# Latent expansion of the second block: three products ahead, one total per tile, stores from the sync engine

## The chip, the cores and the metric

The kernel runs on one core of a Trainium2 chip. The metric is the device time of one execution in microseconds. Five engines take part: TensorE (PE, with PEld for its weight loads), VectorE (DVE), ScalarE (ACT), GpSimd (POOL) and the sync engine (SP), which only issues DMAs here. A name with a q (ACTq, SPq) is an issue of a DMA by that engine.

## The reference, cut to what matters

The program is two transformer blocks over 1024 tokens of width 1024. The change touches one part of the second block, the expansion of the latent attention's queries and keys (four heads):

```python
q = (_rmsnorm_2(c_q, q_a_norm_w) @ w_uq).reshape(b, s, MLA_HEADS, MLA_QK)       # MLA_QK = 128 + 64
q_nope, q_rope = q[..., :MLA_NOPE], q[..., MLA_NOPE:]
q_rope = q_rope * cos + _rotate_half(q_rope) * sin
kv = (_rmsnorm_2(c_kv, kv_a_norm_w) @ w_ukv).reshape(b, s, MLA_HEADS, MLA_NOPE + MLA_V)
k_nope, v_mla = kv[..., :MLA_NOPE], kv[..., MLA_NOPE:]
k_rope = broadcast over the heads of (k_rope * cos + _rotate_half(k_rope) * sin)
q_m = _rmsnorm_2(concatenate([q_nope, q_rope]), mla_q_norm_w)
k_m = _rmsnorm_2(concatenate([k_nope, k_rope]), mla_k_norm_w)
o_mla = _mla_attention(q_m, k_m, v_mla)
```

So each of the eight (head, query or key) pairs needs a product of 128 features x 1024 tokens, the sum of squares over its 128 plain and 64 rotated features, the inverse root of that sum, and two scalings.

## The kernel before

All engines run programs of their own and meet at semaphores. Everything is laid out features first: a tile is 128 partitions (features) x 1024 tokens. Float32 products are made of three rounded products (high x high, low x high, high x low; lines 523 to 525), so a tile with one K block is 6 matmuls of 512 columns and one with two K blocks is 12. PSUM is used as four slots of 128 x 1024, `wide(0)` to `wide(3)`.

The stage before this one makes the rotated parts of the queries (`q_rope`, two tiles, each with two heads) and of the keys (`k_rope`), and the values `v_value`; ACT issues the stores of the values (line 1524), then squares the two tiles of `q_rope` (line 1527). `k_rope_sq` was made earlier.

The latent expansion then runs over e = 0 to 7: head e // 2, key tile for even e (one K block, weights `ukv`), query tile for odd e (two K blocks, weights `uq_nope`).

- TensorE: `expand(e)` makes the product in slot e % 2; from e = 2 it waits until tile e - 2 has been scaled out of it (`g_free`). `head_total(e)` adds over the features with a matrix of ones: the squared product `tmp[e % 2]`, and then the rotated squares with a matrix that picks 64 partitions (`halves`), into slot 2 + e % 2 (line 561). The order is product 0, then total 0, product 1, total 1, product 2 and so on.
- ACT: `head_square(e)` (line 1535) squares the product; then come the logarithm of the total (line 1549) and its exponential (line 1555), which give the inverse root `g_rms`. Between these, ACT issues the stores of tile e - 1 (lines 1541 and 1542) and does the square of e + 1.
- DVE: scales the product out of PSUM to `g_nope` (line 2018) and the rotated part to `g_rope` (line 2022). From e = 2 on it waits for the store of tile e - 2, which used the same buffer.
- SP: after the weight slabs it waits for the stores of the values and of both parts of head 0 (`g_stored[e] >= 32 * hd + 32`), and loads head 0 from memory into `head_raw` in seven DMAs (line 380); the loads of the next heads follow as POOL has split the ones before.
- POOL: when all seven have landed, ten operations split head 0 into high and low parts (lines 496 and 500).

The attention starts when head 0 is split (TensorE, `logits(0)`, ten matmuls a unit) and when all stores of the expansion have landed (DVE waits for `g_stored` at 128 ahead of its first maximum, line 2029).

## Time and profile before

| | us |
|---|---|
| median of the runs (lowest, highest) | 3333.71 (3331.11, 3339.38) |
| the profiled execution | 3333.93 |
| its span | 3332.1 |
| TensorE, busy in the span | 3149.4 (95%) |
| DVE | 1506.8 (45%) |
| POOL | 1176.7 (35%) |
| ACT | 824.1 (25%) |
| share of TensorE in the chain that ended last | 88% |
| latent expansion, from the first value store (2114.76) to the first maximum (2192.62) | 77.9 |

The span is the time from the first to the last instruction of the core. A busy TensorE is not a TensorE at its peak; its granted clock is told as a share of 2.4 GHz (0.50 is 1.2 GHz), its mean over the span is 0.977. The chain that ended last goes back from the last instruction, at each step to what released it. In a row by stretch stand its start and end, its length, the busy time of PE, PEld, DVE, ACT and POOL with the number of instructions, the mean granted clock, the share of time that the DMA engines were busy (of 1), and GB/s. The share of an engine in the whole span says little on this stage: the rows of the stage itself are what is to be read.

### The profile page before, as it was taken

Reading aid. Unit: us, or ns where it says so; the run is one execution under the profiler, and the core shown is the slowest. Engines: PE = TensorE matmul, PEld = TensorE weight load, DVE = VectorE, ACT = ScalarE, POOL = GpSimd, SP = SyncE. Lnnn points to the kernel's source line nnn. Section 1 sums busy time; section 2 is a strip of 40 time slices with the busy share of each in tenths; the row PEclk is TensorE's granted clock in tenths of the full one; section 3 lists DMA queues with packets and bytes.
Section 4 is the critical chain, followed back from the end, with each engine's and each line's share of the span. In section 5 each row is a group of like instructions: output and inputs, shape, how many; then the busy total and the mean of one; then the engine's idle time right before and its main releaser. Section 6 shows DMA issues by size and latency. Waiting matters only on the chain.

```text
span 3332.1 us, 34809 instructions
## 1 busy us (share of the span) xinstructions
PE 3149.4 (95%) x13566; PEld 2462.9 (74%) x13566; DVE 1506.8 (45%) x2220; ACT 824.1 (25%) x1194; POOL 1176.7 (35%) x559
## 2 busy tenths in 40 slices
PE   7999998999988899999999799889998999999999
PEld 5788785678765688888887477568666788888887
DVE  3799956554443522121223521355984423223226
ACT  3322205511334201001001332245774100001001
POOL 2254333334422234334333133273002444444443
PEclk9899999999999999999999899999999999999999
DMA  2022310034200011111111122442421111111112
GB/s 104 26 89 96 141 48 7 1 131 157 78 26 26 26 51 47 48 50 45 50 50 44 34 86 97 139 139 67 111 83 60 39 51 48 47 50 45 49 50 76
DMA packets 69272, 217.54 MB, mean 65 GB/s; under 512 B 7468, under 2 KB 18900, under 8 KB 68408
## 3 DMA queue, kind: packets, MB, share of 16 engines
q1 hardware_dynamic: 40832, 145.51, 14.1%
q10 hardware_dynamic: 28344, 70.74, 5.8%
q8 instruction: 62, 1.02, 0.1%
q14 instruction: 34, 0.28, 0.0%
HBM read 175.31 MB, written 40.65 MB: 65 GB/s over the span
## 4 chain that ended last, share of the span: by engine, by line
PE 88%; DVE 5%; ACT 4%; issue 1%; POOL 1%; ACTq 0%; DMA 0%; POOLq 0%; DVEq 0%
PE ps L523 26%; PE ps L525 25%; PE ps L524 25%; PE ps L561 3%; PE ps L724 2%; PE ps L1047 1%; PE ps L1035 1%; PE ps L714 1%; PE ps L1020 1%; POOL w_lo L419 1%; DVE x L1720 1%; DVE y L1719 1%; PE ps L1021 1%; POOL w_hi L416 0%; ACT mprobs L1423 0%
## 5 line engine op out<-in xcount | busy, mean ns | idle before, releaser
L416 POOL TENSOR_TENSOR w_hi<-w_raw,zero 128x1024 fp32r<-128x1024 f32 x202 | 385.4, 1908 | 1785.5 <-PE ps L525 1778.8
L523 PE MATMUL ps<-normed_hi,w_hi 128*128 128x512 f32 x1488 | 588.5, 395 | 34.7 <-DVE normed_lo L1704 18.2
L524 PE MATMUL ps<-normed_lo,w_hi 128*128 128x512 f32 x1488 | 583.6, 392 | 0.0
L525 PE MATMUL ps<-normed_hi,w_lo 128*128 128x512 f32 x1488 | 583.1, 392 | 0.0
L419 POOL TENSOR_TENSOR w_lo<-w_raw,w_hi 128x1024 fp32r<-128x1024 f32 x202 | 537.6, 2661 | 15.9
L523 PEld LDWEIGHTS ps<-normed_hi,w_hi 128*128 128x128 f32 x1488 | 282.2, 190 | 100.4 <-issue 28.6
L523 PE MATMUL ps<-hidden_hi,w_hi 128*128 128x512 f32 x864 | 336.9, 390 | 2.8 <-DVE hidden_lo L1944 2.8
L525 PE MATMUL ps<-hidden_hi,w_lo 128*128 128x512 f32 x864 | 336.8, 390 | 0.0
L524 PE MATMUL ps<-hidden_lo,w_hi 128*128 128x512 f32 x864 | 336.6, 390 | 0.0
L524 PEld LDWEIGHTS ps<-normed_lo,w_hi 128*128 128x128 f32 x1488 | 282.2, 190 | 60.6 <-issue 2.2
L525 PEld LDWEIGHTS ps<-normed_hi,w_lo 128*128 128x128 f32 x1488 | 282.1, 190 | 59.3
L523 PE MATMUL ps<-h_hi,w_hi 128*128 128x512 f32 x528 | 208.8, 395 | 8.3 <-DVE h_lo L1704 5.0
L524 PE MATMUL ps<-h_lo,w_hi 128*128 128x512 f32 x528 | 207.6, 393 | 0.0
L525 PE MATMUL ps<-h_hi,w_lo 128*128 128x512 f32 x528 | 207.4, 393 | 0.0
L1942 DVE TENSOR_TENSOR tmp<-tmp,ps 128x1024 f32<-128x1024 f32 x22 | 26.9, 1221 | 369.0 <-PE ps L525 367.5
L523 PEld LDWEIGHTS ps<-hidden_hi,w_hi 128*128 128x128 f32 x864 | 162.6, 188 | 37.0 <-DVE hidden_lo L1944 3.2
L525 PEld LDWEIGHTS ps<-hidden_hi,w_lo 128*128 128x128 f32 x864 | 162.5, 188 | 33.9
L524 PEld LDWEIGHTS ps<-hidden_lo,w_hi 128*128 128x128 f32 x864 | 162.6, 188 | 33.7
L2156 DVE TENSOR_TENSOR y<-y,ps 128x1024 f32<-128x1024 f32 x64 | 78.1, 1220 | 206.6 <-PE ps L525 205.6
L1778 DVE MATCH_REPLACE8 score<-top,score 128x1024 f32<-128x1024 f32 (+2 forms) x192 | 167.9, 889 | 0.0
L1774 DVE MAX8 top<-score 128x8 f32<-128x1024 f32 (+2 forms) x192 | 162.2, 893 | 0.0
L2148 DVE TENSOR_TENSOR tmp<-tmp 128x1024 f32<-128x1024 f32 x32 | 59.6, 1861 | 220.1 <-ACT tmp L1678 220.1
(366 smaller groups left out, 5171.5 us busy)
## 6 DMA issues: line engine op xcount, KB each, us to landing
w_raw<-weights_dram SPq DMA_DIRECT2D x228, 512.0 KB, 3.6
gates_scratch<-tmp ACTq DMA_DIRECT2D x24, 512.0 KB, 2.7
gated<-gates_scratch ACTq DMA_DIRECT2D x24, 512.0 KB, 5.6
head_part<-diff_qk_scratch SPq DMA_DIRECT2D x48, 256.0 KB, 6.4
x_in<-x_dram ACTq DMA_DIRECT2D x4, 1024.0 KB, 10.9
x<-x_dram ACTq DMA_DIRECT2D x1, 4096.0 KB, 14.6
diff_qk_scratch<-d_hi ACTq DMA_DIRECT2D x8, 512.0 KB, 2.7
diff_qk_scratch<-d_out ACTq DMA_DIRECT2D x8, 512.0 KB, 2.7
```

The lines of the kernel that those rows point to most:

```text
L416: nc.gpsimd.tensor_tensor(w_hi[s][:], raw[s][:], zero[:, 0:1].broadcast_to([P, 1024]), ALU.add).then_inc(w_rounded, 1)
L419: nc.gpsimd.tensor_tensor(w_lo[s][:], raw[s][:], w_hi[s][:].bitcast(F32), ALU.subtract).then_inc(w_split, 1)
L523: nc.tensor.matmul(out, sh, mh, start=start, stop=False)
L524: nc.tensor.matmul(out, sh, ml, start=False, stop=False)
L525: return nc.tensor.matmul(out, sl, mh, start=False, stop=stop)
L561: last = nc.tensor.matmul(out[:, n:n + HALF], lhs, src[:, n:n + HALF], start=start, stop=stop)
L714: last = nc.tensor.transpose(ps[:, 4 + n_tr % 2, q * P:(q + 1) * P], mix_rows[group % 2][q][:, j * P:(j + 1) * P], ident[:])
L724: nc.tensor.matmul(ps[:, 6 + group % 2, :], value[:, j, :], probs_t[n_tr % 2][:], start=j == 0, stop=j == group // 2).then_inc(pv_done, 1)
L1774: nc.vector.max(top8[:, e, :], sc).then_inc(dve_step, 1)
L1778: nc.vector.match_replace(sc, top8[:, e, :], sc, TAKEN).then_inc(dve_step, 1)
L2148: tt(part[:], part[:], part[:], ALU.mult).then_inc(u_sq, 1)
L2156: tt(y[:, m, :], y[:, m, :], wide(m % 4), ALU.add).then_inc(u_added, 1)
```

## The change

TensorE makes products 0, 1 and 2 ahead of the first total and product e + 3 after total e. The products go to the slots 0, 1 and 3 in turn (`G_SLOTS`), all totals to slot 2; product e + 3 waits until tile e is scaled out, total e + 1 until the logarithm of e has been taken. DVE adds the rotated squares to 64 partitions of the squared tile (`rope_summed`), so a total is one pass with the ones (four matmul records in place of eight). ACT issues no stores here any more: it does logarithm, exponential and the square of e + 2. SP issues the stores of the values, of tiles 0 to 3, then (when all of these have landed) the loads of head 0, then the stores of tiles 4 to 7, and the loads of the heads 1 to 3 when all have landed.

```diff
--- before.py
+++ after.py
@@ -86,6 +86,7 @@
...
+G_SLOTS = (0, 1, 3)
...
@@ -337,6 +338,7 @@
         g_done, g_sq, g_tot, g_rs, g_free, g_roped = (
             sem("mla_" + n) for n in ("tile", "squared", "total", "inverse", "nope_out", "rope_out"))
         r_done, r_free = sem("rope_done"), sem("rope_free")
+        g_summed, g_log = sem("mla_rope_summed"), sem("mla_log")
         g_stored = [sem(f"mla_stored{i}") for i in range(2)]
...
@@ -364,11 +366,25 @@
 
             load_slabs(2, SLABS["out_2"][0] + 2)
 
+            sp.wait_ge(v_act, 4)
+            sp.wait_ge(v_dve, 4)
+            for hd in range(MLA_HEADS):
+                sp.dma_start(t["mla_v"][hd], v_value[:, :, hd * P:(hd + 1) * P]).then_inc(v_stored, 16)
+
+            def store_parts(e):
+                hd, is_q = e // 2, e % 2
+                n, r0 = MLA_HEADS * (1 - is_q) + hd, ROPE * (hd % 2) if is_q else 0
+                sp.wait_ge(g_roped, e + 1)
+                sp.dma_start(t["mla_nope"][n], g_nope[e % 2][:]).then_inc(g_stored[e % 2], 16)
+                sp.dma_start(t["mla_rope"][n], g_rope[e % 2][r0:r0 + ROPE, :]).then_inc(g_stored[e % 2], 16)
+
+            for e in range(4):
+                store_parts(e)
             sp.wait_ge(v_stored, 16 * MLA_HEADS)
             sp.wait_ge(dv_stored, 16 * DIFF_HEADS)
             for hd in range(MLA_HEADS):
                 for e in range(2):
-                    sp.wait_ge(g_stored[e], 32 * hd + 32)
+                    sp.wait_ge(g_stored[e], 64 if hd == 0 else 32 * MLA_HEADS)
...
@@ -378,6 +394,9 @@
                     for e, part in enumerate(src):
                         rows_of = slice(0, P) if len(src) == 1 else slice(64 * e, 64 * e + 64)
                         sp.dma_start(head_raw[n][rows_of, :], part).then_inc(heads_in, 16)
+                if hd == 0:
+                    for e in range(4, 2 * MLA_HEADS):
+                        store_parts(e)
...
@@ -965,30 +984,27 @@
             def expand(e):
 
                 hd, is_q = e // 2, e % 2
-                if e >= 2:
-                    pe.wait_ge(g_free, e - 1)
+                if e >= 3:
+                    pe.wait_ge(g_free, e - 2)
                 s = SLABS["uq_nope" if is_q else "ukv"][0]
                 if e == 1:
                     pe.wait_ge(w_split, s + 1)
                 parts, kt = (cq, 2) if is_q else (ckv, 1)
-                tile(s % 2, hd * kt * P, parts, kt, e % 2).then_inc(w_used if hd == MLA_HEADS - 1 else g_done, 1)
+                tile(s % 2, hd * kt * P, parts, kt, G_SLOTS[e % 3]).then_inc(w_used if hd == MLA_HEADS - 1 else g_done, 1)
 
             def head_total(e):
 
-                pe.wait_ge(g_sq, e + 1)
-                if e == 0:
-                    pe.wait_ge(rope_sq, 3)
-                hd, is_q = e // 2, e % 2
-                over_features(wide(2 + e % 2), tmp[e % 2], ones[:], True, False)
-                rope = q_rope_sq[:, hd // 2, :] if is_q else k_rope_sq[:]
-                over_features(wide(2 + e % 2), rope, halves[:, 1 + (hd % 2 if is_q else 0), :],
-                              False, True).then_inc(g_tot, 1)
-
-            expand(0)
+                pe.wait_ge(g_summed, e + 1)
+                if e:
+                    pe.wait_ge(g_log, e)
+                over_features(wide(2), tmp[e % 2], ones[:]).then_inc(g_tot, 1)
+
+            for e in range(3):
+                expand(e)
             for e in range(2 * MLA_HEADS):
                 head_total(e)
-                if e + 1 < 2 * MLA_HEADS:
-                    expand(e + 1)
+                if e + 3 < 2 * MLA_HEADS:
+                    expand(e + 3)
 
 
 
@@ -1520,8 +1536,6 @@
                 nc.scalar.activation(v_value[:, j, :], ps[:, j, :], ACT.Copy).then_inc(v_act, 1)
             act.wait_ge(v_act, 4)
             act.wait_ge(v_dve, 4)
-            for hd in range(MLA_HEADS):
-                act.dma_start(t["mla_v"][hd], v_value[:, :, hd * P:(hd + 1) * P]).then_inc(v_stored, 16)
             for p in range(2):
                 act.wait_ge(r_free, p + 1)
                 nc.scalar.activation(q_rope_sq[:, p, :], q_rope[:, p, :], ACT.Square).then_inc(rope_sq, 1)
@@ -1532,28 +1546,21 @@
             def head_square(e):
                 act.wait_ge(*((w_used, SLABS["uq_nope" if e % 2 else "ukv"][0] + 1) if e // 2 == MLA_HEADS - 1
                               else (g_done, e + 1)))
-                nc.scalar.activation(tmp[e % 2][:], wide(e % 2), ACT.Square).then_inc(g_sq, 1)
-
-            def store_parts(e):
-                hd, is_q = e // 2, e % 2
-                n, r0 = MLA_HEADS * (1 - is_q) + hd, ROPE * (hd % 2) if is_q else 0
-                act.wait_ge(g_roped, e + 1)
-                act.dma_start(t["mla_nope"][n], g_nope[e % 2][:]).then_inc(g_stored[e % 2], 16)
-                act.dma_start(t["mla_rope"][n], g_rope[e % 2][r0:r0 + ROPE, :]).then_inc(g_stored[e % 2], 16)
+                if e >= 2:
+                    act.wait_ge(g_tot, e - 1)
+                nc.scalar.activation(tmp[e % 2][:], wide(G_SLOTS[e % 3]), ACT.Square).then_inc(g_sq, 1)
 
             head_square(0)
+            head_square(1)
             for e in range(2 * MLA_HEADS):
                 act.wait_ge(g_tot, e + 1)
                 if e >= 2:
                     act.wait_ge(g_roped, e - 1)
-                step(nc.scalar.activation(g_rms[e % 2][:], wide(2 + e % 2), ACT.Ln, bias=eps[:],
-                                          scale=1.0 / (P + ROPE)))
-                if e:
-                    store_parts(e - 1)
-                if e + 1 < 2 * MLA_HEADS:
-                    head_square(e + 1)
+                nc.scalar.activation(g_rms[e % 2][:], wide(2), ACT.Ln, bias=eps[:], scale=1.0 / (P + ROPE)).then_inc(g_log, 1)
+                act.wait_ge(g_log, e + 1)
                 nc.scalar.activation(g_rms[e % 2][:], g_rms[e % 2][:], ACT.Exp, scale=-0.5).then_inc(g_rs, 1)
-            store_parts(2 * MLA_HEADS - 1)
+                if e + 2 < 2 * MLA_HEADS:
+                    head_square(e + 2)
...
@@ -2009,18 +2016,30 @@
                 dve.wait_ge(v_done, j + 1)
                 nc.vector.tensor_copy(v_value[:, j, :], ps[:, j, :]).then_inc(v_dve, 1)
 
+            def rope_summed(e):
+                hd, is_q = e // 2, e % 2
+                r0 = ROPE * (hd % 2) if is_q else 0
+                rope = q_rope_sq[r0:r0 + ROPE, hd // 2, :] if is_q else k_rope_sq[0:ROPE, :]
+                dve.wait_ge(g_sq, e + 1)
+                tt(tmp[e % 2][r0:r0 + ROPE, :], tmp[e % 2][r0:r0 + ROPE, :], rope, ALU.add).then_inc(g_summed, 1)
+
+            dve.wait_ge(rope_sq, 3)
+            rope_summed(0)
+            rope_summed(1)
             for e in range(2 * MLA_HEADS):
                 hd, is_q = e // 2, e % 2
                 dve.wait_ge(g_rs, e + 1)
                 if e >= 2:
                     dve.wait_ge(g_stored[e % 2], 32 * (e // 2))
                 which = "mla_q" if is_q else "mla_k"
-                stt(g_nope[e % 2][:], wide(e % 2), col(which + "_nope"), g_rms[e % 2][:], ALU.mult,
+                stt(g_nope[e % 2][:], wide(G_SLOTS[e % 3]), col(which + "_nope"), g_rms[e % 2][:], ALU.mult,
                     ALU.mult).then_inc(g_free, 1)
                 r0 = ROPE * (hd % 2) if is_q else 0
                 rope = q_rope[r0:r0 + ROPE, hd // 2, :] if is_q else k_rope[0:ROPE, :]
                 stt(g_rope[e % 2][r0:r0 + ROPE, :], rope, col(which + "_rope")[r0:r0 + ROPE, :],
                     g_rms[e % 2][r0:r0 + ROPE, :], ALU.mult, ALU.mult).then_inc(g_roped, 1)
+                if e + 2 < 2 * MLA_HEADS:
+                    rope_summed(e + 2)
```

## Rows read from the trace of the kernel before

**Rows 1.** The chain that ended last, 2100 to 2215: start us, us, what.

```profile
2122.63 6.71 PE ps L561 x8
...
2133.25 3.71 PE ps L561 x8
...
2169.05 5.40 PE ps L561 x8
...
2188.14 4.40 DMA mla_rope_scratch<-g_rope
2192.62 1.24 DVE mstat L2029
```

**Rows 2.** Busy time by stretch; granted clock, DMA share, GB/s come last.

```profile
2118.50:2128.60 10.10, 5.97 (x7) 2.52 (x8) 0.00 (x0) 2.91 (x3) 0.00 (x0) 0.50 0.49 139
2128.70:2169.60 40.90, 32.05 (x98) 17.67 (x97) 14.01 (x10) 18.16 (x18) 7.41 (x4) 1.00 0.51 157
2169.70:2173.00 3.30, 3.30 (x6) 1.23 (x5) 3.03 (x2) 0.24 (x1) 3.22 (x2) 0.50 0.21 45
```

**Rows 3.** Timeline of ACT: start us, us, engine, line, operation, [idle before <-releaser].

```profile
2114.76 4.86 ACTq L1524 DMA_DIRECT2D mla_v_scratch<-v_value  x4
...
2129.37 1.11 ACT L1549 ACTIVATE g_rms<-ps,eps 128x1024 f32<-128x1024 f32 x1 [6.80 <-PE ps L561]
...
2133.09 1.05 ACT L1555 ACTIVATE g_rms<-g_rms 128x1024 f32<-128x1024 f32 x1
...
2145.00 0.33 ACTq L1541 DMA_DIRECT2D mla_nope_scratch<-g_nope  x1
...
2151.42 1.11 ACT L1549 ACTIVATE g_rms<-ps,eps 128x1024 f32<-128x1024 f32 x1 [2.85 <-PE ps L561]
```

**Rows 4.** Timeline of TensorE in the expansion.

```profile
2140.12 1.98 PE L561 MATMUL ps<-tmp,ones 128*128 128x512 f32 x4 [1.78 <-ACT tmp L1535]
...
2169.05 3.21 PE L561 MATMUL ps<-tmp,ones 128*128 128x512 f32 x4 [1.91 <-ACT tmp L1535]
...
2174.51 0.39 PE L524 MATMUL ps<-cq_lo,w_hi 128*128 128x512 f32 x1
...
2176.80 0.39 PE L525 MATMUL ps<-cq_hi,w_lo 128*128 128x512 f32 x1
```

**Rows 5.** Timeline of DVE in the expansion.

```profile
2134.18 1.28 DVE L2018 SCALAR_TENSOR_TENSOR g_nope<-ps,cols,g_rms 128x1024 f32<-128x1024 f32 x1 [19.51 <-ACT g_rms L1555]
2135.38 1.27 DVE L2022 SCALAR_TENSOR_TENSOR g_rope<-k_rope,cols,g_rms 64x1024 f32<-64x1024 f32 x1
...
2164.18 2.83 DVE L2022 SCALAR_TENSOR_TENSOR g_rope<-k_rope,cols,g_rms 64x1024 f32<-64x1024 f32 x1
```

**Rows 6.** Timeline of SP: the first loads of head 0.

```profile
2148.93 0.81 SPq L380 DMA_DIRECT2D head_raw<-mla_nope_scratch  x2
```

**Rows 7.** Timeline of POOL: first and last splits of head 0, first of head 1.

```profile
2162.20 8.43 POOL L496 TENSOR_TENSOR head_part<-head_raw,zero 128x1024 fp32r<-128x1024 f32 x4 [49.08 <-DMA head_raw<-mla_v_scratch]
...
2184.16 2.35 POOL L500 TENSOR_TENSOR head_part<-head_raw,head_part 128x1024 fp32r<-128x1024 f32 x1
2190.37 7.45 POOL L496 TENSOR_TENSOR head_part<-head_raw,zero 128x1024 fp32r<-128x1024 f32 x4 [3.85 <-DMA head_raw<-mla_v_scratch]
```

**Rows 8.** Timeline of TensorE: first and tenth matmul of the first logits.

```profile
2186.66 0.69 PE L523 MATMUL ps<-head_part,head_part 128*128 128x512 f32 x1 [4.65 <-POOL head_part L500]
...
2190.39 0.39 PE L1010 MATMUL ps<-head_part,head_part 128*128 128x512 f32 x1
```

**Rows 9.** Timeline of ACT: logarithm and exponential back to back, an earlier stage.

```profile
1966.15 1.12 ACT L1501 ACTIVATE d_rms<-ps,eps 128x1024 f32<-128x1024 f32 x1 [2.08 <-PE ps L561]
1967.30 1.06 ACT L1503 ACTIVATE d_rms<-d_rms 128x1024 f32<-128x1024 f32 x1
```

**Rows 10.** DMA queues, 2148.9 to 2162.3: packets, MB, share (q1 SP, q10 ACT).

```profile
q1 hardware_dynamic: 752, 2.62, 73.2%
q10 hardware_dynamic: 290, 1.06, 20.8%
```

## The prediction

> **What bounds the kernel now.** I read the 40 slices and the chain that ended last first: TensorE carries 88% of the chain, so a change elsewhere moves the time only where TensorE stands still. The latent expansion is such a stretch. I then read the chain of waits between 2100 and 2200 us, and after it the timeline of each engine there. The reader is to see two chains that run side by side and meet at the first row maximum of the attention.
>
> The first chain makes the tiles. For each of the eight tiles (e = 0 to 7, keys at even e, queries at odd e) it is: product, square (ACT), total (eight matmul records, 3.71 us at the full clock), logarithm and exponential (ACT), scaling (DVE), store. The logarithm of tile 0 starts at 2129.37, that of tile 3 at 2151.42 [rows 3], that of tile 7 at 2182.05. After it the last store is issued by ACT and takes 4.40 us to land, and DVE, which waits for all stores, starts the first maximum at 2192.62 [rows 1].
>
> The second chain makes head 0. SP waits until the stores of tiles 0 and 1 have landed, issues seven loads from 2148.93 on [rows 6], and POOL starts its ten splits when the last has landed, at 2162.20, and ends them at 2184.16 + 2.35 = 2186.51 [rows 7]. TensorE waits 4.65 us for that and starts the logits at 2186.66; the tenth matmul, with which the first unit is whole, starts at 2190.39 [rows 8], so the unit is there at some 2190.9. The second chain thus ends only 1.7 us before the first (2192.62). That decides the case: what shortens the tile chain is worth 1.7 us at most, unless head 0 comes earlier as well.
>
> **The change part by part.**
> *Start.* ACT no longer issues the stores of the values, four issues in 4.86 us [rows 3]; SP does, which has nothing due then. TensorE has products 0, 1 and 2 to do from 2114.8: 24 matmuls at 0.23 us (ten of them span 2176.80 - 2174.51 = 2.29 us [rows 4]) = 5.5 us, so until 2120.3. Meanwhile ACT does the rotated squares (2 x 1.0), square 0 until 2117.8, and DVE adds the rotated squares. That addition on 64 x 1024 isn't in the trace; I take the 64 x 1024 row, 1.27 us [rows 5] (bounds 1.2 and, as with POOL at work, 2.83 [rows 5]), so it ends at 2119.1, hidden by products 1 and 2. Total 0 starts at 2120.3. It now has four matmul records instead of eight: half of 3.71 is 1.86, and with 0.15 for the end of the pipeline, which is not halved, the logarithm follows 2.0 us later, at 2122.3. That is 7.1 us earlier than in the kernel before.
>
> *Cycle of a tile.* The wait on g_free stands ahead of product e + 3, and on TensorE's queue total e + 1 stands behind that product. g_free for it comes from the scaling of tile e. So with the full clock one cycle is: total to logarithm 2.0; logarithm to exponential 1.15 (1967.30 - 1966.15 [rows 9]); exponential to scaling 1.09 (2134.18 [rows 5] - 2133.09 [rows 3]); the scaling 1.28 [rows 5] and 0.05 to TensorE; then the product, 12 matmuls = 2.8 for a query tile, 6 = 1.4 for a key tile. Together 8.4 with a query product, 7.0 with a key product. Before, a cycle was (2151.42 - 2129.37)/3 = 7.35 on average [rows 3]: exponential and scaling lay beside the next square and total. The halved total is paid back by a longer loop. Squares e + 2 (1.0) and the additions of e + 2 (1.27) lie in TensorE's idle stretch and cost nothing; without that cover they would add 2.3 a tile. Products of the cycles 0, 1 and 2 are tiles 3, 4, 5 (query, key, query): 8.4 + 7.0 + 8.4 = 23.8, so logarithm 3 starts at 2146.1, 5.3 us earlier than before.
>
> *Clock.* In each cycle TensorE is idle from the end of total e to product e + 3: 0.15 + 1.15 + 1.09 + 1.33 = 3.7 us and some. After an idle stretch of 1.91 us that followed a short product [rows 4] the granted clock fell to 0.50, that is 1.2 GHz [rows 2], and a total took 5.40 instead of 3.71: +1.7. After the 6.2 us idle at the start it was 0.50 too and the total took 6.71: +3.0 [rows 1, 2]. Where the idle stretches were shorter, 1.78 us at most [rows 4], the clock stayed at 1.00, 2.4 GHz [rows 2]. An idle stretch of 3.7 lies between the two prices; in proportion 1.7 + 1.3 x 1.8/4.3 = 2.3 a cycle (bounds 0, and all work of the cycle at half speed: +1.7 + 1.4 = 3.1 or +1.7 + 2.8 = 4.5). Three cycles: 6.9. Logarithm 3 starts at 2153.0.
> The Trainium skill (TensorE: Matmul & The Clock Gate, section "Why this matters for your kernels") names idle gaps between bursts of matmuls as what puts the clock back to half rate. It speaks against this change, and the trace agrees with the 0.50 stretches above; with the rule left aside the sum would end 6.9 us lower.
>
> *Head 0.* Rope part of tile 3 ready: 2153.0 + 1.15 + 1.09 + 2.47 (scaling start to rope end, 2135.38 + 1.27 - 2134.18 [rows 5]) = 2157.7. SP issues the store at once. Now the first loads need both semaphores at 64, that is tiles 0 to 3 landed, no longer 0 and 1. From the issue of a store pair to the first load were 2148.93 - 2145.00 = 3.93 us [rows 3, 6]: loads start at 2161.7, 12.7 us later than before. They took 2162.20 - 2148.93 = 13.3, but of 3.68 MB moved in that time 1.06 MB were stores on the other queue [rows 10]; without these, 13.3 x 2.62/3.68 = 9.5, and with latency I take 10.5 (bounds 9.5 and 13.3). The later stores are issued by SP behind the loads and don't stand in their way. POOL starts at 2172.2. Its ten splits took 24.3 beside DVE's work; for head 1, with DVE less busy, the first four took 7.45 instead of 8.43 [rows 7], by which ten would take 21.5. Tiles 5 to 7 are scaled beside them here too, so 24.3 (bounds 21.5 and 24.5): 2196.5. Logits to the first maximum 4.4 (2190.9 - 2186.5, at the low clock as before): 2200.9. Against 2192.62 that is +8.3 us.
>
> *The last stores.* Stores 4 to 7 queue behind 2.6 MB of loads, and scaling 6 waits for store 4. With loads landed at 2172, store 4 lands near 2175, tile 7 is scaled near 2186 and lands near 2190: 10 us before the logits, so free, unless the loads take some 10 us longer. ACT's 0.8 us of store issues in each cycle go too, but they were in the tile chain, which the loop above replaces.
> The Trainium skill (Trainium Kernel Development and Optimization, section "Key Constraints") says that issuing from another engine saves only the sequencer's issue time. By it the move to SP is worth the 4.86 us at the front and no transfer time; the sum has no more than that.
>
> After the first maximum the kernel is the same, and POOL's head 1 keeps its distance from head 0, so the shift passes to the end. Profiled execution 3333.93 (span 3332.1 and 1.8 around it) + 8.3 = 3342.2; the median of the runs, 3333.71, is 0.2 below, so 3342.
>
> **Rivals.**
> *A, warm clock and short loads: no change.* Clock stays at 1.00 (-6.9), POOL undisturbed (-2.8): 8.3 - 9.7 = -1.4, 3332.5. For it: idle stretches of up to 1.78 us did not lower the clock. Against: the one of 1.91 did, and after the one of 4.65 ten matmuls start over 3.7 us, where the full clock needs 2.3 [rows 4, 8].
> *B, cold throughout.* The clock never comes back in the three cycles: 4.5 + 3.1 + 4.5 = 12.1 instead of 6.9, +13.5: 3347.3. For it: nearly the whole of the first total ran before the clock rose [rows 1, 2]. Against: it rose within 3.5 us of unbroken work at 2169.7 to 2173.0 [rows 2].
> *C, faster.* The last store stays the late one, and head 0 is ready before it. At the full clock tile 7 is stored and landed near 2180, 12.8 us earlier: 3321. It needs POOL to end by 2175, so rope part 3 by about 2137; the point from which C decides lies 14 us before even the fully clocked loop (2150.8). Only loads that do not wait for tiles 2 and 3 would give it.
> *D, the queue of SP turns late.* Stores behind loads delay scaling 6 and 7 until the last landing is later than the logits; from 10 us on more than reckoned each further us counts. 3350.
>
> **How the numbers follow.** Forecast (3337 to 3346) 0.60, A (3332 to 3337) 0.18, B 0.12, C 0.04, D 0.06. A difference of 0.3% (10 us) is about what a measurement can tell from no change: slower by more means above 3343.9. That takes B, D and a quarter of the forecast's chance, 0.32; faster is C, 0.04; within 0.3% is the rest, 0.64. For 8 in 10 the range leaves out C, some of A and most of D: 3333 to 3348.
>
> **What would show it.** Right: logarithm 0 at about 2122; TensorE idle 3.7 us and more in each of the first five cycles "until DVE scaling"; the granted clock at 0.50 in several stretches of 2120 to 2175; loads of head 0 first issued near 2162; POOL's first split near 2172; the first maximum waiting for TensorE, not for a DMA, near 2201. Wrong: a clock of 1.00 throughout (then A), first loads before 2155, or a maximum that still waits for a store (then D or C).

## The result, and the profile after

| | before | after |
|---|---|---|
| median of 20 runs each, us | 3333.72 (3327.92 to 3339.38) | 3341.74 (3334.92 to 3344.84) |
| ratio | 1 | 1.0022 (95% interval 1.0015 to 1.0029), +7.3 us (+5.0 to +9.7) |
| profiled execution, us | 3333.93 (span 3332.1) | 3338.95 (span 3337.3) |

The changed kernel is a little slower, within the 0.3% that the prediction called no change. Both traces were laid on the issue of the first store of the values (2114.76 before, 2109.53 after), since the stage begins at different times under the same code ahead of it. In us from there:

| event | before | predicted | after |
|---|---|---|---|
| logarithm of tile 0 | 14.6 | 7.5 | 7.5 |
| logarithm of tile 3 | 36.7 | 38.2 | 34.2 |
| first loads of head 0 | 34.2 | 46.9 | 43.0 |
| POOL's first split | 47.4 | 57.4 | 54.5 |
| POOL done with head 0 | 71.8 | 81.7 | 79.7 |
| last store landed | 77.8 | 75 | 74.7 |
| first maximum | 77.9 | 86.1 | 84.6 |

The timeline of TensorE in after (start us, us, line, operation, idle before and what ended it) answers to [rows 4, 8]:

```profile
2120.63 0.79 PE L542 MATMUL ps<-cq_hi,w_hi 128*128 128x512 f32 x1 [3.61 <-DVE g_nope L2035]
...
2130.31 0.75 PE L542 MATMUL ps<-ckv_hi,w_hi 128*128 128x512 f32 x1 [3.61 <-DVE g_nope L2035]
...
2147.26 0.64 PE L542 MATMUL ps<-ckv_hi,w_hi 128*128 128x512 f32 x1 [3.61 <-DVE g_nope L2035]
...
2171.73 3.47 PE L580 MATMUL ps<-tmp,ones 128*128 128x512 f32 x4 [5.47 <-DVE tmp L2024]
...
2189.37 0.76 PE L542 MATMUL ps<-head_part,head_part 128*128 128x512 f32 x1 [14.17 <-POOL head_part L519]
```

Each product e + 3 stands 3.61 us idle for the scaling of tile e (five such rows, two left out), and the logits wait 14.17 us for POOL, where before they waited 4.65 [rows 8]. The timeline of ACT answers to [rows 3]: logarithm 0 comes 7.1 us nearer to the value store (experiment 5 shows that the stores on SP do that by themselves, with the full totals), and the loop then gives some of it back.

```profile
2117.06 1.11 ACT L1559 ACTIVATE g_rms<-ps,eps 128x1024 f32<-128x1024 f32 x1 [2.05 <-PE ps L580]
...
2126.74 1.11 ACT L1559 ACTIVATE g_rms<-ps,eps 128x1024 f32<-128x1024 f32 x1 [6.57 <-PE ps L580]
...
2143.68 1.11 ACT L1559 ACTIVATE g_rms<-ps,eps 128x1024 f32<-128x1024 f32 x1 [5.25 <-PE ps L580]
```

Busy time by stretch, after (stretch and its length; PE, PEld, DVE, ACT, POOL busy; then granted clock, DMA share, GB/s), answers to [rows 2]. The clock is below 1.00 in four of these five:

```profile
2117.00:2127.00 10.00, 6.09 (x17) 3.94 (x16) 3.60 (x3) 3.34 (x4) 0.00 (x0) 0.83 0.37 115
2127.00:2137.00 10.00, 4.97 (x10) 2.83 (x10) 3.69 (x3) 4.47 (x5) 0.00 (x0) 0.83 0.25 79
2137.00:2147.00 10.00, 4.75 (x16) 2.93 (x16) 4.69 (x4) 4.51 (x5) 0.00 (x0) 1.00 0.25 79
2147.00:2157.00 10.00, 6.13 (x13) 3.76 (x14) 5.20 (x6) 3.08 (x3) 0.00 (x0) 0.69 0.60 193
2157.00:2167.00 10.00, 7.96 (x19) 4.41 (x17) 2.82 (x3) 3.79 (x4) 2.98 (x2) 0.79 0.83 227
```

Timeline of SP, after (to [rows 6]): the store of tile 3's rope part, and 3.6 us behind it the first loads. Then the first loads of head 1, which waited for the last store:

```profile
2148.91 0.45 SPq L379 DMA_DIRECT2D mla_rope_scratch<-g_rope  x1
2152.49 0.80 SPq L396 DMA_DIRECT2D head_raw<-mla_nope_scratch  x2
...
2184.20 0.80 SPq L396 DMA_DIRECT2D head_raw<-mla_nope_scratch  x2
```

Timeline of POOL, after (to [rows 7]); head 0's ten splits last from 2164.01 to 2189.23, 25.2 us:

```profile
2164.01 9.41 POOL L515 TENSOR_TENSOR head_part<-head_raw,zero 128x1024 fp32r<-128x1024 f32 x4 [56.11 <-DMA head_raw<-mla_v_scratch]
...
2186.89 2.34 POOL L519 TENSOR_TENSOR head_part<-head_raw,head_part 128x1024 fp32r<-128x1024 f32 x1
2196.87 7.45 POOL L515 TENSOR_TENSOR head_part<-head_raw,zero 128x1024 fp32r<-128x1024 f32 x4 [7.65 <-DMA head_raw<-mla_v_scratch]
```

Timeline of DVE, after (to [rows 5]); the first maximum now waits for TensorE, where in [rows 1] it followed the landing of the last store:

```profile
2112.56 1.22 DVE L2024 TENSOR_TENSOR tmp<-tmp,k_rope_sq 64x1024 f32<-64x1024 f32 x1 [3.11 <-ACT tmp L1551]
...
2166.48 2.36 DVE L2039 SCALAR_TENSOR_TENSOR g_rope<-q_rope,cols,g_rms 64x1024 f32<-64x1024 f32 x1
2168.86 2.81 DVE L2024 TENSOR_TENSOR tmp<-tmp,q_rope_sq 64x1024 f32<-64x1024 f32 x1
2171.70 1.28 DVE L2035 SCALAR_TENSOR_TENSOR g_nope<-ps,cols,g_rms 128x1024 f32<-128x1024 f32 x1
...
2194.11 1.22 DVE L2048 TENSOR_REDUCE mstat<-ps 128x1 f32<-128x1024 f32 x1 [13.89 <-PE ps L1026]
```

### The profile page after: what moved, and what is told of

Its sections match the earlier page's. It is cut to its first block, busy times and chain, and to the rows that moved or that the text cites. A ratio compares the mean times of both kernels' runs of the same rounds, so it can differ in the third digit from the quotient of the medians.

```text
span 3337.3 us, 34759 instructions
## 1 busy us (share of the span) xinstructions
PE 3140.3 (94%) x13534; PEld 2459.8 (74%) x13534; DVE 1516.3 (45%) x2228; ACT 824.3 (25%) x1194; POOL 1177.4 (35%) x559
## 4 chain that ended last, share of the span: by engine, by line
PE 88%; DVE 5%; ACT 3%; POOL 2%; issue 1%; DMA 1%; SPq 0%; ACTq 0%; POOLq 0%; DVEq 0%
PE ps L542 26%; PE ps L543 25%; PE ps L544 25%; PE ps L580 2%; PE ps L743 2%; PE ps L1063 1%; PE ps L1051 1%; PE ps L733 1%; PE ps L1036 1%; POOL w_lo L438 1%; DVE x L1727 1%; DVE y L1726 1%; PE ps L1037 1%; POOL w_hi L435 0%; ACT mprobs L1439 0%
```

## The experiments

The theory (the prediction's): in after, the stage ends with head 0's chain, gated on tiles 2 and 3, and the order of TensorE's queue with the idle stretches and the clock sets when these come. Rivals: the gate alone; the queue order alone, the clock being harmless; the stores on SP.

**1. The gate alone.** Head 0's loads wait for tiles 0 and 1 only; the rest of after stays.

```diff
-            for e in range(4):
+            for e in range(2):
                 store_parts(e)
...
-                    sp.wait_ge(g_stored[e], 64 if hd == 0 else 32 * MLA_HEADS)
+                    sp.wait_ge(g_stored[e], 32 if hd == 0 else 32 * MLA_HEADS)
...
-                    for e in range(4, 2 * MLA_HEADS):
+                    for e in range(2, 2 * MLA_HEADS):
```

> The changed kernel, but SP issues the stores of tiles 0 and 1, then (both landed) the seven loads of head 0, then the stores of tiles 2 to 7. Theory: head 0's loads wait for tiles 2 and 3, and POOL's chain behind them ends last. Loads then start about 26 us after the first value store instead of 43, POOL ends near 64 and the chain of tiles, unchanged, becomes the late one: its last store lands near 75, so the first maximum comes at 75 instead of 84.6. Time about 3332, 9 to 10 below the changed kernel. Rival 1: the longer loop of a tile alone makes the loss, the gate on tiles 2 and 3 is harmless: the first maximum stays near 84 and the time at 3341.

Measured: 3340.41, ratio 1.0029 (1.0018 to 1.0039). The stage did what was expected: loads at 2135.77, 25.8 after the value store, POOL at 2147.34, the first maximum 74.6 after it (75 expected), 10 us earlier than in after. The time did not follow. Timelines of TensorE and of POOL in this kernel:

```profile
2217.92 0.79 PE L542 MATMUL ps<-head_part,head_part 128*128 128x512 f32 x1 [8.66 <-POOL head_part L519]
```

```profile
2196.21 7.45 POOL L515 TENSOR_TENSOR head_part<-head_raw,zero 128x1024 fp32r<-128x1024 f32 x4 [21.88 <-DMA head_raw<-mla_v_scratch]
```

POOL stood idle for 21.88 us, since head 1's loads come behind all eight stores (2184.55), and TensorE waited 8.66 us for head 1. The gate is what makes head 0's chain end the stage in after, but head 1 stood right behind it. This term was missing from the theory.

**2. The queue order alone.** Total e + 1 goes ahead of the product: product e + 2 follows total e + 1, and the gate stays.

```diff
-                if e + 3 < 2 * MLA_HEADS:
-                    expand(e + 3)
+                if 1 <= e < 2 * MLA_HEADS - 2:
+                    expand(e + 2)
```

> The changed kernel, but product e + 3 stands behind total e + 1 on TensorE's queue, not ahead of it (order: products 0, 1, 2, totals 0, 1, product 3, total 2, product 4 ...). Theory: the queue order makes the loop of a tile 7 to 8.4 us; with it undone ACT (3.2) and DVE (3.8) bound it, 4.0 to 4.5 a tile. Rope part 3 is ready near 25 us after the first value store instead of 39, loads start at 29, the first maximum comes at 67 to 71. Time 3324 to 3328, below the kernel before. Rival 2: the loop is bound by the work of DVE and ACT or by the clock, not by the order: a cycle of 7 or more stays, time within 3 us of 3341.

Measured: 3327.25, 0.9975 (0.9965 to 0.9985). From logarithm to logarithm 4.04 us on average instead of 8.3, the clock 0.99 to 1.00 from 2117 to 2147, loads 28.2 and first maximum 67.7 after the value store. Timeline of TensorE:

```profile
2120.01 0.50 PE L542 MATMUL ps<-cq_hi,w_hi 128*128 128x512 f32 x1 [0.36 <-DVE g_nope L2035]
```

and of DVE:

```profile
2150.14 1.28 DVE L2035 SCALAR_TENSOR_TENSOR g_nope<-ps,cols,g_rms 128x1024 f32<-128x1024 f32 x1 [7.51 <-DMA mla_rope_scratch<-g_rope]
```

The product in front of the total is what costs: 3.61 us idle becomes 0.36, and the whole is 14 us faster than after and faster than before. These 14 us hold both the order and the clock that rises with it; experiment 4 tells them apart. The 7.51 us are the mechanism of rival D (a store queued behind 2.6 MB of loads holds a scaling); here nothing that ends the stage waits for that tile.

**3. Both edits of 1 and 2 together.**

```diff
-            for e in range(4):
+            for e in range(2):
                 store_parts(e)
...
-                if e + 3 < 2 * MLA_HEADS:
-                    expand(e + 3)
+                if 1 <= e < 2 * MLA_HEADS - 2:
+                    expand(e + 2)
```

> Both edits: loads of head 0 behind stores 0 and 1, and total e + 1 ahead of product e + 3. Theory: loads start near 20 us after the first value store, POOL's chain ends near 58, the first maximum comes near 63; the stores of tiles 2 and 3, queued behind the loads, hold the scaling of tiles 4 and 5 back by some 7 us, but the last store still lands near 49. Time about 3320, the least of all. Rival 1 (gate harmless): no better than the total-first kernel alone, 3324 to 3328. Rival 3: store and load traffic collide, scaling 4 to 7 come so late that the last store ends the stage: 3326 or more.

Measured: 3327.7, 0.9984 (0.9975 to 0.9993); not the 3320 expected. The first maximum came 62.6 after the value store (63 expected), then TensorE waited 5.43 us for head 1 (2202.15). The same term as in 1: what is won ahead of head 0 is worth nothing beyond head 1's chain. But head 1 was late here by another way. Timeline of DVE, the scaling of tile 4:

```profile
2142.67 1.28 DVE L2035 SCALAR_TENSOR_TENSOR g_nope<-ps,cols,g_rms 128x1024 f32<-128x1024 f32 x1 [7.72 <-DMA mla_rope_scratch<-g_rope]
```

It waited 7.72 us for the store of tile 2, which stood behind head 0's loads, and in this kernel that wait lies in the chain that ended last: it holds back the tiles behind it, the last store and with it head 1's loads, which start at 2167.49, 58.0 us after the value store (51.2 in 2).

**4. The clock alone.** After, with nine matmuls put into each cycle's idle stretch; their results are overwritten.

```diff
+                    pe.wait_ge(g_log, e + 1)
+                    s = SLABS["ukv" if e % 2 else "uq_nope"][0] % 2
+                    for n in range(9):
+                        nc.tensor.matmul(wide(2)[:, n % 2 * HALF:n % 2 * HALF + HALF], w_hi[s][:, 0:P],
+                                         ckv[0][:, 0, 0:HALF], start=True, stop=True)
```

> The changed kernel with nine extra matmuls of 512 columns after each of totals 0 to 4, into the slot of the totals once its logarithm has been taken, so that TensorE is idle for 1.3 us in a cycle instead of 3.6 (their results are overwritten by the next total). Theory: the idle stretches make the clock fall; with the filler it stays at 1.00, cycles are 8.4 and 7.0 us, logarithm 3 comes 31.3 us after the first value store instead of 34.1 (and instead of up to 38 in other executions). Time 3 to 6 below the changed kernel, 3336 to 3339. Rival 4: the clock costs nothing here or does not respond: 3341 to 3342, or more because product e + 3 now queues behind the filler.

Measured: 3336.11, 1.0004 (0.9995 to 1.0013), 5.6 less than after. Busy time by stretch, of the ones that stood at 0.83 and 0.69 in after:

```profile
2127.00:2137.00 10.00, 8.29 (x27) 4.51 (x25) 3.75 (x4) 3.51 (x4) 0.00 (x0) 1.00 0.42 137
...
2147.00:2157.00 10.00, 8.67 (x32) 5.51 (x31) 6.60 (x6) 4.14 (x5) 0.00 (x0) 1.00 0.46 138
```

The cycles became 8.36, 7.01, 8.35, 7.02, 8.35: the 8.4 and 7.0 that the prediction worked out for the full clock. The loop's price has two parts, the order of the queue and the clock. The clock is 5.6 us by the two medians, 5.2 when each is taken against its own runs of before; in this profiled execution the stage is 3.8 us shorter than in after (80.8).

**5. The stores on SP alone.** Before, with its full totals and its order; only the stores are issued by SP, the loads of head 0 still behind tiles 0 and 1, head 1's between the later stores.

```diff
+            for hd in range(MLA_HEADS):
+                sp.dma_start(t["mla_v"][hd], v_value[:, :, hd * P:(hd + 1) * P]).then_inc(v_stored, 16)
...
+            for e in range(2):
+                store_parts(e)
...
+                    for e in ({0: (4,), 2: (5,), 4: (6, 7)}.get(i, ()) if hd == 1 else ()):
+                        store_parts(e)
...
-                act.dma_start(t["mla_v"][hd], v_value[:, :, hd * P:(hd + 1) * P]).then_inc(v_stored, 16)
...
-                if e:
-                    store_parts(e - 1)
```

> The kernel before, with only the stores moved from ACT to SP: values; tiles 0 and 1; loads of head 0; tiles 2 to 4; loads of head 1 with the stores of tiles 5, 6 and 7 between them. Order of products and totals, squares and slots as before. Theory: 4.9 us go at the start and 0.65 to 0.86 in each cycle with a key product, loads of head 0 start 7 us earlier, so the first maximum comes 70 to 71 us after the first value store instead of 77.9, and head 1 is in time: 3326 to 3327, 7 below the kernel before. Rival: stores that queue behind 2.6 MB of loads hold the scaling of tile 4 and later ones back, and the last store or head 1 ends the stage: 3331 or more.

Measured: 3323.98, 0.9974 (0.9963 to 0.9985), and a first maximum 66.3 after the value store; both are earlier than expected. Timeline of TensorE, the first half of total 0:

```profile
2111.91 1.98 PE L580 MATMUL ps<-tmp,ones 128*128 128x512 f32 x4 [1.30 <-ACT tmp L1552]
```

Logarithm 0 comes 6.7 us after the value store instead of 14.6. That is 4.86 of issues [rows 3] and 3.0 of clock: the first total no longer stands behind 6 us of idleness and has the full clock, where it took 6.71 instead of 3.71 [rows 1]. The expectation had left out these 3.0. From logarithm 0 to logarithm 7 it is 49.2 us instead of 52.7, which is the rest of the 11.5 us that the stage is shorter. This part of the change, alone, makes the kernel faster, and logarithm 0 comes earlier than in after (7.5), where the total is halved but two more products stand ahead of it.

**6. The halved totals alone.** Before, with the addition on DVE and totals of four records; stores stay on ACT.

```diff
-                pe.wait_ge(g_sq, e + 1)
...
-                over_features(wide(2 + e % 2), tmp[e % 2], ones[:], True, False)
...
+                pe.wait_ge(g_summed, e + 1)
+                over_features(wide(2 + e % 2), tmp[e % 2], ones[:]).then_inc(g_tot, 1)
...
+                if e + 1 < 2 * MLA_HEADS:
+                    rope_summed(e + 1)
```

> The kernel before, with only the rotated squares added by DVE and one pass per total. Here the addition stands in the chain between square and total. Theory: a total is 1.86 shorter and 1.3 longer by the addition, 0.55 a tile; TensorE's idle stretches grow from 1.1 to 1.8 to 2.5 to 3.1 us, and the clock falls in part of the cycles at 1.7 or more a time. At the full clock 3329; with a clock that falls in half of the seven cycles about 3333; so 3329 to 3335, no gain that is clear. Rival: the shorter total is worth its 1.86 us in each tile, 3320 to 3326.

Measured: 3339.22, 1.0016 (1.0007 to 1.0025), slower, against 3329 to 3335 expected. Timeline of TensorE, two totals:

```profile
2139.51 3.78 PE L562 MATMUL ps<-tmp,ones 128*128 128x512 f32 x4 [3.03 <-DVE tmp L2012]
2149.52 1.98 PE L562 MATMUL ps<-tmp,ones 128*128 128x512 f32 x4 [2.37 <-DVE tmp L2012]
```

Busy time by stretch, this kernel, and below it the same stretches of before:

```profile
2137.00:2147.00 10.00, 7.49 (x16) 4.44 (x16) 3.60 (x3) 3.08 (x3) 0.00 (x0) 0.66 0.44 144
2157.00:2167.00 10.00, 7.31 (x21) 4.03 (x19) 4.98 (x5) 3.08 (x3) 6.95 (x4) 0.84 0.61 204
```

```profile
2137.00:2147.00 10.00, 7.78 (x26) 4.45 (x24) 2.47 (x2) 4.59 (x5) 0.00 (x0) 1.00 0.37 127
2157.00:2167.00 10.00, 8.88 (x29) 5.02 (x27) 5.05 (x3) 4.20 (x4) 4.80 (x3) 1.00 0.67 230
```

The addition comes between square and total, so TensorE stands idle for 2.4 to 3.1 us where it was 1.1 to 1.9 (two of them in [rows 4]). Of the seven totals after the first, the two behind 2.37 and 2.42 us of idleness took 1.98 and 1.99, the two behind 2.69 and 2.74 took 2.76 and 2.84, the three behind 3.00 to 3.09 took 3.57 to 3.78. There a total of half the matmuls takes as long as the whole one at the full clock (3.71), and the granted clock is 0.66 where it was 1.00. The three longest stretches all stand behind a key product, which has half the matmuls of a query product, so in this loop the length of the stretch and the work ahead of it cannot be told apart. POOL's splits took 27.0 us instead of 24.3, but the first maximum waits for the last store here, so the tile chain ends the stage.

**7. Early loads, with head 1 in time.** As 1, and head 1's loads are issued between the stores of tiles 4 to 7.

```diff
-                    sp.wait_ge(g_stored[e], 64 if hd == 0 else 32 * MLA_HEADS)
+                    sp.wait_ge(g_stored[e], min(32 * hd + 32, 128))
...
+                    for e in ({0: (4,), 4: (5, 6)}.get(i, ()) if hd == 1 else ()):
+                        store_parts(e)
```

> The early-loads kernel (changed kernel, head 0's loads behind stores 0 and 1), with the loads of head 1 no longer behind the stores of tiles 5 to 7 but between them, and waiting for tiles 2 and 3 alone. Theory: the early loads brought the first maximum 10 us forward, and that was lost because TensorE reached head 1's logits before POOL had split head 1 (8.7 us). With head 1 in time the gain passes to the end: 3331 to 3333. Rival: the gain is lost elsewhere, in clock or in the attention: 3339 to 3341 as with early loads alone.

Measured: 3332.28, 0.9993 (0.9983 to 1.0002). Head 1's splits end 18.8 us after the first maximum (2187.68), and TensorE has no wait for POOL behind it. The 8 us that 1 lost are back: head 1 was their cause.

**8. POOL's chain shortened.** As 2, and the ten splits of head 0 are done by ACT (five copies) and DVE (five differences).

```diff
-            for hd in range(MLA_HEADS):
+            for hd in range(1, MLA_HEADS):
...
+            act.wait_ge(heads_in, heads_landed(1))
+            for n, dst in ((0, 0), (1, 2), (3, 6), (4, 7), (2, 4)):
+                nc.scalar.activation(head_parts[0][dst][:], head_raw[n][:], ACT.Copy).then_inc(g_log, 1)
...
+                tt(p[lo][lanes, :], head_raw[n][lanes, :], p[hi][lanes, :].bitcast(F32), ALU.subtract).then_inc(head_split, 1)
```

> The total-first kernel, with the ten splits of head 0 done by ACT (five roundings) and DVE (five differences), which stand idle then, instead of by POOL. Theory: POOL's 23.5 us for head 0 is what ends the stage there; shared it ends some 9 to 10 us earlier, the first maximum comes 58 us after the first value store instead of 67.7, and then head 1 on POOL is just about in time (1 to 2 us late): 3317 to 3320. Rival: head 1, whose loads wait for all stores and for these splits, takes the whole gain back: 3325 to 3328.

Measured: 3317.13 (3314.35 to 3320.02), 0.9953 (0.9940 to 0.9967): the best kernel of the study, 16 us faster than before. Timelines of ACT and DVE:

```profile
2148.29 4.84 ACT L1567 ACTIVATE head_part<-head_raw 128x1024 fp32r<-128x1024 f32 x5 [1.36 <-DMA head_raw<-mla_v_scratch]
```

```profile
2155.22 6.37 DVE L2057 TENSOR_TENSOR head_part<-head_raw,head_part 128x1024 fp32r<-128x1024 f32 x5
```

From 2148.29 to 2161.6 it is 13.3 us (11.2 of work, the rest is DVE ending tiles 6 and 7), where POOL took 23.5 in 2. The first maximum is 10.1 us earlier than in 2, TensorE waits 2.0 us for head 1, which it did not in 2, and the median is 10.1 us lower than in 2.

**9. The clock in the halved kernel.** As 6, with eight matmuls between each product and the total behind it; their results are overwritten.

```diff
+                    if e:
+                        pe.wait_ge(g_rs, e)
+                    for n in range(8):
+                        nc.tensor.matmul(wide(2 + (e + 1) % 2)[:, n % 2 * HALF:n % 2 * HALF + HALF], cq[0][:, 0, 0:P],
+                                         ckv[0][:, 0, 0:HALF], start=True, stop=True)
```

> The kernel with the halved totals alone, and eight extra matmuls of 512 columns between product e + 1 and total e + 1, into the slot which that total then overwrites, so that TensorE is idle for 0.6 to 1.2 us in a cycle instead of 2.4 to 3.1. Theory: the halved totals alone lost 6 us only because the longer idle stretches let the clock fall; with the filler it stays at 1.00, a cycle is some 6.3 to 7.0 us, and the time is 3329 to 3331, below the kernel before. Rival: the loss comes from DVE's addition in the chain or from DVE and POOL beside each other; then the filler changes nothing, 3336 to 3340.

Measured: 3335.86, 1.0001 (0.9992 to 1.0010), 3.4 less than 6, but not the 3329 to 3331 expected. The intervals of 6 and 9 meet, so the difference is not quite clear of noise. Against the runs of before on each run's own chip it is 4.4: +6.0 in 6, +1.6 here. Where the filler closed the gap the clock was 1.00; behind the one stretch of 3.05 us that it left, a total took 2.90. Timeline of TensorE:

```profile
2162.49 1.98 PE L562 MATMUL ps<-tmp,ones 128*128 128x512 f32 x4 [0.56 <-DVE tmp L2017]
2170.78 2.90 PE L562 MATMUL ps<-tmp,ones 128*128 128x512 f32 x4 [3.05 <-DVE tmp L2017]
```

Timeline of POOL, first and last splits of head 0, 27.2 us instead of before's 24.3 [rows 7]:

```profile
2163.07 9.41 POOL L497 TENSOR_TENSOR head_part<-head_raw,zero 128x1024 fp32r<-128x1024 f32 x4 [47.98 <-DMA head_raw<-mla_v_scratch]
...
2187.03 3.20 POOL L501 TENSOR_TENSOR head_part<-head_raw,head_part 128x1024 fp32r<-128x1024 f32 x1
```

The first maximum waits for TensorE, and that for POOL; in 6 it waited for the last store. So the clock is most of what the halved totals cost: 2.0 of the 2.5 us of the stage and 4.4 of the 6.0 us of the medians. That the rest is POOL's splits beside DVE's added instructions rests on these rows; no run took it away by itself, and by the interval above it can also be nothing.

**All together.** "Stage" is the time from the value store to the first maximum, plus TensorE's wait for head 1, less before's 77.9; "median" is the difference of the medians to the runs of before on the same chip (the ratios above weigh all runs and can lie up to 3 us from it).

| kernel | stage | median |
|---|---|---|
| after | +6.7 | +8.0 |
| 1 gate | -3.2 + 8.7 | +7.1 |
| 2 order | -10.2 | -6.0 |
| 3 both | -15.3 + 5.4 | -5.6 |
| 4 clock | +2.9 | +2.8 |
| 5 stores on SP | -11.5 | -9.2 |
| 6 halved totals | +2.5 | +6.0 |
| 7 gate, head 1 in time | -5.5 | -0.9 |
| 8 order, shared splits | -20.3 + 2.0 | -16.1 |
| 9 halved, filled | +0.5 | +1.6 |

The stage explains the order of the times, but for 4 and 6, which change places. The medians lie some 2.5 us higher on average than the stage says. Before's one profiled execution is the shortest behind the stage: from the first maximum to the end it took 1139.5 us, the other ten, waits for head 1 left out, 1140.1 to 1144.7. Whether that is this one execution or the kernel, one profile of each cannot tell.

## Why the prediction was right, step by step

The forecast was 3342 and the median 3341.74. That they meet so closely is in part luck: the stage grew by 6.7 us, not by 8.3, in a sum whose errors partly cancel, and the medians differ by 1.3 us more than the stage does. The mechanism is what the runs bear out.

*What bounds the stage.* Right. Two chains met, and that of head 0 ends the stage in after: POOL's last split, the logits, the maximum waiting for TensorE. Experiments 7 and 1 show the gate to be the cause: undone, the stage is 10 to 12 us shorter.

*The start.* Right to 0.1 us: logarithm 0 at 7.5. The addition on 64 x 1024 took 1.22 (1.27 taken); beside POOL 2.81 (bound 2.83).

*The cycle.* Right: idle stretches of 3.61 (3.7 predicted), and 8.4 and 7.0 us at the full clock, as experiment 4 shows.

*The clock.* The mechanism was right, the term was mis-sized: 2.3 a cycle. Against experiment 4 the first three cycles of after (9.68, 8.58, 8.36) pay 1.3, 1.6 and 0.0, 2.9 us instead of 6.9. The 2.3 was interpolated between a 1.91 us and a 6.2 us stretch as if each cycle paid; two of three did, and these two less than 2.3 (the interpolation itself gives 2.2; 0.2 of the 6.9 us is rounding). The 0.50 named as a sign was there, from 2120.70 to 2123.30 and from 2130.40 to 2133.40. The fourth and fifth cycles paid 1.6 and 2.4, but lie behind tile 3, for which the loads wait. By medians the clock costs 5.2 to 5.6 us (experiment 4), so one profile doesn't settle this term.
The Trainium skill (TensorE: Matmul & The Clock Gate, section "Why this matters for your kernels") advises that idle gaps between bursts of matmuls be avoided so as not to lose the full rate. Experiments 4 and 9 agree: with the stretches filled, 5.2 and 4.4 us came back, each against its own runs of before. But in after the clock was 1.00 from 2137 to 2147 although the product there stood behind 3.61 us of idleness like the others.

*The loads.* 8.7 us from logarithm 3 to the first load were worked out, 8.8 measured. The transfers took 11.5 instead of 10.5. "The later stores don't stand in their way" was not quite so. DMA queues of after from 2152.4 to 2164.1 (packets, MB, share):

```profile
q1 hardware_dynamic: 846, 3.01, 92.3%
```

3.01 MB moved, 0.39 more than the loads' 2.62: the stores of tile 4, issued behind them at 2157.00, shared the engines.

*POOL and the logits.* 25.2 instead of 24.3, 4.9 instead of 4.4.

*Signs of being wrong.* One was "first loads before 2155", and they came at 2152.49. It was written in before's time: laid on the value store it is 40.2 us, and the loads came at 43.0, so the sign did not appear; the whole stage began 5.2 us earlier.

*The sum.* -4.1 (cycles) + 0.1 + 1.0 (loads) + 0.9 (POOL) + 0.5 (logits) = -1.6: 84.6 instead of 86.1. The stage is thus 6.7 us longer than before. The profiled pair differs by 5.2 us in span: +6.7 in the stage, -5.2 ahead of it, +3.7 behind it.

*What is behind the stage.* Of the 3.7 one place can be read. Timeline of TensorE at the output projection and busy time of the 10 us that follow, first before, then after:

```profile
2514.84 0.77 PE L523 MATMUL ps<-o_all_hi,w_hi 128*128 128x512 f32 x1 [3.67 <-DVE o_all_lo L2116]
```

```profile
2515.00:2525.00 10.00, 10.00 (x33) 6.96 (x33) 3.29 (x3) 6.21 (x7) 0.00 (x0) 0.86 0.14 51
```

```profile
2516.81 0.77 PE L542 MATMUL ps<-o_all_hi,w_hi 128*128 128x512 f32 x1 [3.67 <-DVE o_all_lo L2135]
```

```profile
2517.00:2527.00 10.00, 10.00 (x29) 7.10 (x30) 2.45 (x2) 4.75 (x6) 0.00 (x0) 0.70 0.13 49
```

The code and the idle stretch (3.67) are the same, the granted clock behind it is 0.86 and 0.70. In the ten kernels besides before this clock is 0.70 to 0.87, and in 6 and 9, which have before's order and stores, it is 0.83 and 0.72. Nothing ties it to the change; no run isolated it, and the 3.7 stay open.

*Head 1.* "POOL's head 1 keeps its distance from head 0" was wrong. Head 1 was split 19.5 us after the first maximum before and 24.5 after it in after, and TensorE comes to it after 24.7 (experiment 1: 2217.92 - 8.66 - 2184.58). The slack fell from 5.2 to 0.1 us. It did no harm here, but it took the gain from experiments 1 and 3. SP's stores were costed as things that load 0 waits for; that load 1 was moved behind all of them wasn't.

*The rivals.* A (the clock stays, POOL undisturbed) gave 3332.5; the warm clock alone is 3336 (experiment 4). B (cold in every cycle) did not come. C asked for loads that don't wait for tiles 2 and 3; experiment 1 gave them and met head 1. D's wait occurs, 7.5 us in experiment 2, where it ends nothing, and in after the last store lands 9.9 us ahead of the first maximum. With loads as early as in experiment 3 it does count: 7.72 us, in the chain that made head 1 late.

The change by its parts, then: stores on SP -9 (5); halved totals with the addition on DVE between square and total +6 (6), of which the clock is the larger part (9); head 0 gated on tile 3, worth -9 when undone with head 1 in time (7); and product e + 3 ahead of total e + 1, worth -14 when undone (2), of which some 5 are the clock (4). The last two overlap, since a faster loop brings tile 3 sooner, and with both undone no more is won, by head 1 (3). So the parts do not add up to the +8.0 of the whole, and what the halved totals are worth in after's own order, where the addition lies under the products, no run shows.

## What to carry to other kernels

On an in-order queue look at what each instruction stands in front of: a product run ahead that needs a buffer freed by the far end of a chain puts the whole chain into the loop, however much work it takes off the engine. Cost idle time of TensorE together with the clock that follows it, since halving work that sits between waits can slow the remainder by as much. When a wait is moved, follow every transfer that is queued behind it to its user, the second head as well as the first.

## What the runs showed of the hardware that was not expected

- Work on DVE and POOL at once slows by operand. In after, beside POOL's splits, the addition took 2.81 instead of 1.22 and the rope scaling, whose inputs both lie in SBUF, 1.43 to 2.36 instead of 1.27, but the scaling that reads PSUM stayed at 1.28 (the DVE rows above). POOL's ten splits took 23.5 us beside the least DVE work (2), 25.2 in after and 27.2 in 9; one difference took 2.34 or 3.20. The Trainium skill (SBUF — State Buffer, section "SBUF: two separate sides") says that a DVE instruction with two SBUF inputs and a GpSimd instruction that reads SBUF exclude each other for the length of one; the runs agree on which instructions are hit.
- The same four matmuls of a total in the loop of 6 took 1.98 us behind 2.4 us of idleness and 3.6 to 3.8 behind 3.0. The length of the stretch alone does not decide it: in after the product at 2138.89 ran at the full clock behind 3.61 us, and in 4 a total took 1.98 us behind 2.80.
- Moving stores to another queue had two sides. The Trainium skill (Trainium Kernel Development and Optimization, section "Key Constraints") says that issuing from several engines saves only the issue time; in 5 the 4.86 us saved brought 3.0 more through the clock, and in 2 and 3 stores that now stood behind loads held DVE for 7.5 and 7.7 us.
- The time of the same code ahead of the stage had two ranges of values, 2108.9 to 2110.0 and 2113.7 to 2116.7 at the first value store, in eleven kernels that are equal up to there. What decides between them stays open.
